# The second block's modulation moved into the first block's attention, and five stores into a mixer

## The chip, the cores and the metric

The kernel runs on one core of a Trainium2 chip. Its time is device microseconds of one execution, from launch to end, as the median of three runs. The profile was taken on a further execution of the same program. TensorE (PE) does the matmuls, VectorE (DVE) and ScalarE (ACT) take the results out of PSUM and do the elementwise work, GpSimd (POOL) helps on data in SBUF, and SyncE (SP) issues the DMA transfers. Each engine works through its own queue in order and waits on semaphores.

## What is computed

Three transformer-like blocks in float32 on 1024 tokens of width 1024. The first block has stick-breaking attention (8 heads of 64) beside a causal pooling, a feed-forward of width 4096 and a per-layer embedding. The second begins with a modulation by a vector c, which is the part that the change moves:

```
# first block
o = stick_breaking_attention(q, k, v)             # sigmoid(z) times a running product of 1 - sigmoid(z)
mixed = concat(rms(o) * g, pooled) @ w_out
x = layer_norm(a * x + mixed)
x = layer_norm(a * x + square(relu(x @ w_up)) @ w_down)
x = layer_norm(a * x + (p @ w_ple) * sigmoid(x @ w_ple_gate))
# second block
mod = silu(c) @ w_ada + b_ada                     # c: 1 x 1024, w_ada: 1024 x 6144
sh_m, sc_m, gt_m, sh_f, sc_f, gt_f = split(mod, 6)
h = rms(x, g_pre_mix) * (1 + sc_m) + sh_m         # first use of mod
...
h = rms(x, g_pre_ffn) * (1 + sc_f) + sh_f
x = x + gt_f * rms(square(relu(h @ w_up)) @ w_down)
```

The third block follows and is not touched.

## The kernel before

The program is a chain of stages, one function each, and all of an engine's instructions stand in the order in which the code writes them; nothing schedules them later. Most matmuls are in three passes on operands split in a high and a low part (lines 130 to 132), with 512 columns moving against 128 x 128 weights.

`embed_attention_1` (from line 3775) does the projections and the attention. The work is cut in 96 parts: a part is 128 queries of one head against up to 512 keys, and parts come in pairs, one for each of two heads. A step of the loop over `i` (a "unit" in the prediction is one part) issues on TensorE, for even `i`, the scores of parts `i` and `i + 1` (line 3961), then the turn, that is the transpose, of part `i - 2` (line 3970), and the values of parts `i - 4` and `i - 3` (line 3981); an odd step has a turn only. Between them, VectorE caps the diagonal block (4201), ScalarE takes two sigmoids (4072, 4073), VectorE scans and multiplies (4210, 4213), and ScalarE copies the turned part out of PSUM (4082). In the first three quarters of the loop, 24 parts each, projections stand between these as well; the last quarter, from part 72, has none. After the loop come two pooled products (3950), the last sums of squares (3990), and the output product in `mix_out_1`.

`feed_forward` (line 529) is the first block's feed-forward in eight parts, each with 8 groups of up and 16 of down. VectorE takes each group out (line 477 for up, 635 for down) and splits operands (119, 124); in the first part it also does the residual of the normalization (253, 254). With `ada` given, GpSimd multiplies w_ada by silu(c) and adds over rows, in 8 column pieces of 768 and two halves each (lines 704 to 716), SyncE loads them (line 557) and stores the eight sums, which still have 128 rows, to HBM.

`per_layer_embedding` (line 1450) loads these sums back and adds their 128 rows on TensorE: 48 matmuls with the ones vector as the single moving column (line 1528), 30 ahead of the first gate product and 18 later; VectorE adds b_ada (1570). VectorE's `take` (1562) multiplies the embedding product (1518) with the gate.

`seven_product_feed_forward` (line 966) does the second block's feed-forward with seven products for eight (Strassen's scheme). Up has 14 pairs of 128 features; the products of a pair are P1, P6, P5, P7, P2, P3, P4, of 12 passes each. VectorE's `w_sums(i)` and `w_low(i)` make the weights of pair `i` (lines 845, 124), `add(i, n)` takes products out and squares them (845, 1196). The first four feature tiles are computed ahead, by `lead_tensor` and `lead_scalar` in the mixer `mix_out_2`. Their blocks and sums are stored to HBM, 14 stores in all (line 988), and `w_sums(1)` waits for all of them, since its scratch lies on two of the blocks. The next chunk of w_up is loaded ahead of these stores (line 995).

Of the kernel before, what the change touches and what calls it, by code (L numbers as in the profile page):

```python
# [5 lines left out]
F32 = mybir.dt.float32  # L6
F32R = mybir.dt.float32r
ALU = mybir.AluOpType
# [3 lines left out]
P = 128  # L12
# [8 lines left out]
ADA = 6 * D // 8  # L21
# [507 lines left out]
def feed_forward(nc, m, F, w_up, w_down, following, tail, x_spill=None, ada=None, split_before=None):  # L529
# [10 lines left out]
    if ada is not None:  # L540
        ada_in, ada_done, ada_out = m.sem("ada_in"), m.sem("ada_done"), m.sem("ada_out")
        ada_step = m.sem("ada_step")
        ada_k = ada.rearrange("(h k p) (j n) -> j h p k n", p=P, h=2, n=ADA)
        ada_w, ada_sum = m.extra[:, 0:4 * ADA].rearrange("p (k n) -> p k n", n=ADA), m.extra[:, 4 * ADA:5 * ADA]
        a_out, m.mod_in = m.mod_spill, m.sem("ple_mod_in")
        m.mod_rows = m.extra[:, 0:5 * ADA].rearrange("p (j n) -> p j n", n=ADA)

    with nc.Block() as block:
        @block.sync
        def _(sp):  # L550
# [4 lines left out]
            def load_ada(j, h):  # L555

                sp.dma_start(ada_w, ada_k[j, h]).then_inc(ada_in, 16)

            def store_ada(j):

                sp.wait_ge(ada_done, 2 * j + 2)
                sp.dma_start(a_out[j], ada_sum).then_inc(ada_out, 16)
            down_dst = F.w_low[1].rearrange("p (k h) n -> p k h n", h=2)
            if ada is not None:
                load_ada(0, 0)
            with sp.Fori(0, parts - 1) as j:
                if ada is not None:
                    sp.wait_ge(ada_done, 2 * j + 1)
                    load_ada(j, 1)
                load(0, base + OUTS * j + UP, F.w_low[0], up_k[:, :, bass.ds(j * COLS + COLS, COLS)])  # L570
                if ada is not None:
                    store_ada(j)
                    load_ada(j + 1, 0)
                load(1, base + OUTS * j + OUTS, down_dst, down_k[j + 1])
            if ada is not None:
                sp.wait_ge(ada_done, 2 * parts - 1)
                load_ada(parts - 1, 1)
                store_ada(parts - 1)
                sp.wait_ge(ada_out, 16 * parts)
                sp.dma_start(m.mod_rows, m.mod_spill[0:5].rearrange("j p n -> p j n")).then_inc(m.mod_in, 16)  # L580
# [115 lines left out]

        if ada is not None:
            @block.gpsimd
            def _(pool):
                def part(j):  # L700
                    for h in range(2):
                        pool.wait_ge(ada_in, 32 * j + 16 * h + 16)
                        c = m.c_act[:, 4 * h:4 * h + 4].unsqueeze(2).broadcast_to([P, 4, ADA])
                        pool.tensor_tensor(ada_w, ada_w, c, ALU.mult).then_inc(ada_step, 1)  # L704
                        pool.wait_ge(ada_step, 5 * j + 2 * h + 1)
                        pool.tensor_tensor(ada_w[:, 0:2], ada_w[:, 0:2], ada_w[:, 2:4], ALU.add).then_inc(ada_step, 1)
                        pool.wait_ge(ada_step, 5 * j + 2 * h + 2)
                        if h == 0:
                            if not (isinstance(j, int) and j == 0):
                                pool.wait_ge(ada_out, 16 * j)  # L710
                            pool.tensor_tensor(ada_sum, ada_w[:, 0], ada_w[:, 1], ALU.add).then_inc(ada_done, 1)
                        else:
                            pool.tensor_tensor(ada_w[:, 0], ada_w[:, 0], ada_w[:, 1], ALU.add).then_inc(ada_step, 1)
                            pool.wait_ge(ada_step, 5 * j + 5)
                            pool.wait_ge(ada_done, 2 * j + 1)
                            pool.tensor_tensor(ada_sum, ada_sum, ada_w[:, 0], ALU.add).then_inc(ada_done, 1)
                part(0)
                with pool.Fori(1, parts) as j:
                    part(j)

class SevenProducts:
# [184 lines left out]

    def lead_vector(self, dve, n):
# [57 lines left out]
def seven_product_feed_forward(nc, m, F, w_up, w_down, following, tail, x_spill):  # L966
# [17 lines left out]
    with nc.Block() as block:  # L984
        @block.sync
        def _(sp):
# [41 lines left out]
            load_chunk(2)  # L1028
            for q in range(2):
                h, pc = F.first_h, F.stage[1]  # L1030
                spill = [F.left_spill[t, q] for t in range(7)]
                sp.wait_ge(F.squared_0, 6 + 2 * q)
                store(F.stored_0, spill[0], h[2 * q][0])
                store(F.stored_0, spill[1], h[2 * q + 1][0])
                store(F.stored_0, spill[2], h[2 * q + 1][1])
# [131 lines left out]
        def _(dve):  # L1167
# [84 lines left out]
            for i in range(F.PAIRS):  # L1252
# [197 lines left out]
def per_layer_embedding(nc, m, a, G, following, V):  # L1450
# [22 lines left out]
    parts_in, mod_done = m.mod_in, m.sem("ple_mod_done")  # L1473
    mod_sets = [(0, 5), (5, 8)]
    mod_rows = m.mod_rows
    n_col = ADA // P
    with nc.Block() as block:
        @block.sync
        def _(sp):
# [5 lines left out]
            sp.wait_ge(mod_done, 1)  # L1485
# [3041 lines left out]
```

## Time and profile before

| | us |
|---|---|
| Median of three runs | 3741.14 |
| Lowest and highest run | 3738.04, 3741.85 |
| Profiled execution | 3736.94 |
| Its span, first to last instruction | 3735.1 |
| TensorE busy in the span | 3520.9 (94%) |
| VectorE busy | 2355.9 (63%) |
| ScalarE busy | 1145.7 (31%) |
| GpSimd busy | 391.6 (10%) |
| Mean granted TensorE clock | 0.972 |

The span is what the profiler saw, the profiled execution's time has the launch and end around it. The granted clock is the share of 2.4 GHz that TensorE got: 1.00 is 2.4 GHz, 0.50 is 1.2 GHz, and a number between is a stretch with both. A matmul's recorded duration is longer than the distance to the next start, because matmuls are pipelined; prices of passes are therefore taken from start to start. "Idle before" in square brackets names what ended an engine's wait.

### The profile page before, as it was taken

To read this page: it belongs to the slowest core of one execution; us is meant where nothing else is said; L and a number is where in the kernel's file an instruction comes from. 1 tells how busy PE (TensorE), PEld (TensorE's weight loads), DVE (VectorE), ACT (ScalarE), POOL (GpSimd) and SP (SyncE) were. 2 spreads that over 40 slices of the span, in tenths; PEclk is the share of its full clock that TensorE was granted. 3 is DMA by queue.
4 is the path that set the end of the run, shared out by engine and by line. 5 is a ranking of instruction groups with operands and counts; after the bars stand their busy time and mean duration, and the time that the engine had idled before them with its cause. 6 is when DMAs were issued, how large, how long until landed. Compare 5 with 4: busy or idle time off the path is not lost. (4 is left out here: it accounts for less than half of the span.)

```text
span 3735.1 us, 42816 instructions
## 1 busy us (share of the span) xinstructions
PE 3520.9 (94%) x16875; PEld 2797.5 (75%) x16875; DVE 2355.9 (63%) x3274; ACT 1145.7 (31%) x2244; POOL 391.6 (10%) x174
## 2 busy tenths in 40 slices
PE   7997898999999989997699999999999999989989
PEld 6664676888888768876677888887777777777687
DVE  7677377555556673999858776768323334446493
ACT  1566230000001352124344224444112223332461
POOL 0113014222331001133100000000000000000000
PEclk9997899999999899999899999999999999999999
DMA  4100212222222121110013436533111221242221
GB/s 168 35 23 23 79 56 84 83 97 109 86 83 99 69 85 54 46 57 23 18 72 125 161 137 216 175 109 145 58 53 60 83 76 59 82 164 97 72 66 76
DMA packets 170935, 323.52 MB, mean 87 GB/s; under 512 B 14992, under 2 KB 45829, under 8 KB 170757
## 3 DMA queue, kind: packets, MB, share of 16 engines
q1 hardware_dynamic: 170756, 321.09, 24.4%
q8 instruction: 119, 1.95, 0.2%
q14 instruction: 60, 0.48, 0.0%
HBM read 248.18 MB, written 72.88 MB: 86 GB/s over the span
## 5 line engine op out<-in xcount | busy, mean ns | idle before, releaser
L130 PE MATMUL banks<-region_parts 128*128 128x512 f32 x2986 | 1195.6, 400 | 40.0 <-DVE region L635 7.5
L132 PE MATMUL banks<-region_parts,weight_chunks_parts 128*128 128x512 f32 x1888 | 739.0, 391 | 0.0
L131 PE MATMUL banks<-region_parts 128*128 128x512 f32 x1802 | 703.8, 391 | 0.0
L130 PEld LDWEIGHTS banks<-region_parts 128*128 128x128 f32 x2986 | 566.8, 190 | 168.3 <-issue 17.9
L132 PE MATMUL banks<-region_parts 128*128 128x512 f32 x1632 | 641.0, 393 | 0.0
L131 PE MATMUL banks<-weight_chunks_parts,region_parts 128*128 128x512 f32 x1536 | 604.7, 394 | 0.0
L132 PEld LDWEIGHTS banks<-region_parts,weight_chunks_parts 128*128 128x128 f32 x1888 | 356.0, 189 | 76.0
L131 PEld LDWEIGHTS banks<-region_parts 128*128 128x128 f32 x1802 | 340.1, 189 | 69.8 <-issue 2.2
L132 PEld LDWEIGHTS banks<-region_parts 128*128 128x128 f32 x1632 | 309.9, 190 | 66.0
L131 PEld LDWEIGHTS banks<-weight_chunks_parts,region_parts 128*128 128x128 f32 x1536 | 293.1, 191 | 63.0 <-issue 4.1
L124 DVE TENSOR_TENSOR region_parts<-region,region_parts 128x512 fp32r<-128x512 f32 (+2 forms) x249 | 266.6, 1072 | 42.1 <-ACT region_parts L848 25.3
L482 ACT ACTIVATE region<-constants 128x512 f32<-128x512 f32 x64 | 40.5, 633 | 618.6 <-DVE constants L477 618.6
L130 PE MATMUL banks<-region_parts,extra_parts 128*128 128x512 f32 x544 | 218.6, 402 | 0.5 <-PEq L984 0.5
L131 PE MATMUL banks<-region_parts,extra_parts 128*128 128x512 f32 x544 | 212.5, 391 | 0.0
L124 DVE TENSOR_TENSOR weight_chunks_parts<-weight_chunks,region_parts 128x1024 fp32r<-128x1024 f32 (+5 forms) x88 | 197.0, 2238 | 2.3
L3220 POOL TENSOR_TENSOR constants<-mask,blocks 128x128 f32<-128x128 f32 x24 | 11.0, 484 | 1672.0 <-DMA b_gate<-in_b_gate 1575.1
L635 DVE TENSOR_TENSOR region<-region,banks 128x512 f32<-128x512 f32 x128 | 85.5, 684 | 148.9 <-PE banks L132 148.6
L2708 DVE CUSTOM_DVE_ANT_0 region<-banks,region 128x128 f32<-128x128 f32 (+7 forms) x64 | 48.5, 758 | 189.9 <-PE banks L2623 135.7
L848 ACT ACTIVATE region_parts<-region 128x512 fp32r<-128x512 f32 (+2 forms) x190 | 118.6, 660 | 145.3 <-DMA region<-left_spill 96.7
L4210 DVE TENSOR_TENSOR_SCAN region<-region,small_numbers 128x512 f32<-128x512 f32 (+3 forms) x96 | 111.6, 1162 | 61.9 <-ACTq L4075 61.9
L1962 DVE SCALAR_TENSOR_TENSOR region<-region,columns 128x1023 f32<-128x1023 f32 (+29 forms) x120 | 149.2, 1330 | 0.0
L704 POOL TENSOR_TENSOR extra<-extra,silu_c 128x3072 f32<-128x3072 f32 x16 | 86.8, 5424 | 570.2 <-DMA extra<-in_w_ada 570.2
(432 smaller groups left out, 5205.3 us busy)
## 6 DMA issues: line engine op xcount, KB each, us to landing
weight_chunks<-in_w_in SPq DMA_DIRECT2D x19, 2048.0 KB, 8.4
weight_chunks<-in_w_up SPq DMA_DIRECT2D x16, 2048.0 KB, 9.3
region<-left_spill SPq DMA_DIRECT2D x98, 256.0 KB, 2.6
extra<-in_w_ada SPq DMA_DIRECT2D x16, 1536.0 KB, 10.8
weight_chunks<-in_w_down SPq DMA_DIRECT2D x9, 2048.0 KB, 7.7
x_spill<-region SPq DMA_DIRECT2D x32, 512.0 KB, 2.6
weight_chunks<-in_w_out SPq DMA_DIRECT2D x8, 2048.0 KB, 8.0
region<-x_spill SPq DMA_DIRECT2D x32, 512.0 KB, 6.2
```

The lines of the kernel that those rows point to most:

```text
L124: return dve.tensor_tensor(m.parts(x), x, m.parts(hi).bitcast(F32), ALU.subtract)
L130: pe.matmul(out, m.parts(lhs[0]), m.parts(rhs[0]), start=first, stop=False, skip_group_check=shared)
L131: pe.matmul(out, m.parts(lhs[0]), m.parts(rhs[1]), start=False, stop=False, skip_group_check=shared)
L132: return pe.matmul(out, m.parts(lhs[1]), m.parts(rhs[0]), start=False, stop=last, skip_group_check=shared)
L482: act.activation(self.h_place(self.h_low, g), self.relu_of, ACT.Square).then_inc(self.squared, 1)
L635: dve.tensor_tensor(x, x, m.bank[:, g % NBANK, :], ALU.add).then_inc(wt.bank_free, 1)
L704: pool.tensor_tensor(ada_w, ada_w, c, ALU.mult).then_inc(ada_step, 1)
L848: act.activation(self.m.parts(hi), x, ACT.Copy).then_inc(sem, 1)
L1962: dve.scalar_tensor_tensor(y, val[:, k, 0:S - lag], m.c("w_dw", (CONV_W - 1 - lag) * 4 + k), y, op0=ALU.mult, op1=ALU.add).then_inc(tap, 1)
L2708: m.dve_link(dve, dve.tensor_tensor_reduce(SB[n % 2][:, 0:w], src, logc[:, (7 - t) * P:(7 - t) * P + w], 1.0, -3e38, ALU.add, ALU.max, x[: ...
L3220: ins = pool.tensor_tensor(bd[t].rearrange("p (b d) -> p b d", d=4), m.mask4.unsqueeze(2).broadcast_to([P, 32, 4]), m.blk[:, t, k:k + 1, : ...
L4210: dve.tensor_tensor_scan(x, x, zeros.broadcast_to([P, w]), kb[:, at + w:at + w + 1], ALU.mult, ALU.add).then_inc(s.scanned, 1)
```

## The change

The modulation leaves the feed-forward and the per-layer embedding. In the attention, w_ada is loaded in 24 pieces of 1024 x 256 into three buffers, one in `extra` and two in the half of the weight buffer that is free by then. A piece is 16 matmuls of 128 x 128 weights with silu(c), 128 x 1, as the moving column, two accumulations of 8. Two pieces stand behind the scores of every even step from part 78 on, four in the last step. VectorE adds b_ada and the gains in one go at the end of the loop, and the last pooled product waits for that, since it uses the same bank. In the second block's feed-forward five of the 14 stores are issued at the end of the mixer, the load of the next chunk of w_up comes behind the other nine, and `w_sums(1)` stands behind `add(0, 2)` instead of ahead of it.

```diff
 def feed_forward(...):          # and all of ada's loads, stores and the block below
-        if ada is not None:
-            @block.gpsimd
-            def _(pool):
-                def part(j):
-                    for h in range(2):
-                        pool.wait_ge(ada_in, 32 * j + 16 * h + 16)
-                        c = m.c_act[:, 4 * h:4 * h + 4].unsqueeze(2).broadcast_to([P, 4, ADA])
-                        pool.tensor_tensor(ada_w, ada_w, c, ALU.mult).then_inc(ada_step, 1)
...
 def per_layer_embedding(...):   # TensorE; DVE's modulation(0), modulation(1) go as well
-            modulation(0)
             for q in range(G.LEAD, 16):
...
-                if q == 5:
-                    modulation(1)
 class SevenProducts:
+    def lead_sync(self, sp):
+        for squares, tile, half in ((1, 0, 0), (2, 1, 0), (3, 2, 0), (4, 3, 0), (6, 1, 1)):
+            sp.wait_ge(self.squared_0, squares)
+            sp.dma_start(self.left_spill[2 if half else tile % 2, tile // 2], self.first_h[tile][half]).then_inc(self.stored_0, 16)
 def mix_out_2(...):             # SyncE
             wt.load(sp, m.wbuf, following[1])
+            F.lead_sync(sp)
 def seven_product_feed_forward(...):
-            load_chunk(2)
             for q in range(2):
...
+            load_chunk(2)
...
                 if i == 0:
                     F.t_low_part(dve, 1, 0, 4)
-                    F.w_sums(dve, 1)
                 add(i, 2)
                 if i == 0:
+                    F.w_sums(dve, 1)
                     F.w_low(dve, 1, range(4))
 def embed_attention_1(...):
+    ADA_BUFS, ADA_PIECES, ADA_FROM = 3, 24, 78
...
+    for n in range(ADA_PIECES):
+        at = ADA_FROM + n // 2 * 2 if n < 22 else NP + 4 - 2
+        ada_at.setdefault((at, 0), []).append(n)
...                              # SyncE, after piece 0 and, once the projections are done, 1 and 2
+            for n in range(ADA_BUFS, ADA_PIECES):
+                sp.wait_ge(s.ada_done, n - ADA_BUFS + 1)
+                load_ada(n)
+            sp.wait_ge(s.ada_done, ADA_PIECES)
             wt.load(sp, m.wbuf, following[1])
...                              # TensorE
+            def modulation(n):
+                if n == 0:
+                    pe.wait_ge(s.c_ready, 1)
+                    pe.wait_ge(wt.bank_free, NBANK + 38)
+                pe.wait_ge(s.ada_in[n % ADA_BUFS], 16 * (n // ADA_BUFS + 1))
+                for t in range(2):
+                    for k in range(NK):
+                        mm = pe.matmul(m.bank[:, 3, 2 * n + t:2 * n + t + 1], ada_w[n % ADA_BUFS][:, k, t * P:(t + 1) * P],
+                                       m.c_act[:, k:k + 1], start=(k == 0), stop=(k == NK - 1), skip_group_check=True)
+                mm.then_inc(s.ada_done, 1)
...
                 if i < NP and i % 2 == 0:
                     scores(i)
                     scores(i + 1)
+                for n in ada_at.get((i, 0), []):
+                    modulation(n)
                 if 2 <= i < NP + 2:
                     turn(i - 2)
...
-            for half in range(2):
-                pooled(3, half, 38 + half)
+            pooled(3, 0, 38)
+            pe.wait_ge(s.mod_read, 1)
+            pooled(3, 1, 39)
...                              # VectorE, after the loop
+            dve.wait_ge(s.ada_done, ADA_PIECES)
+            dve.tensor_tensor(m.mod, m.bank[:, 3, 0:48], m.cols("b_ada", 0, 48), ALU.add).then_inc(s.mod_read, 1)
```

On TensorE, two steps of the attention's last quarter, parts 90 to 93, stood so before (L3961 are scores, L3970 turns, L3981 values; x8 are eight matmuls in a row):

```order
L3961 MATMUL banks<-region 128x512 x2
L3970 MATMUL banks<-constants,region 128x128 x3
L3981 MATMUL banks<-region 64x128 x8
L3970 MATMUL banks<-constants,region 128x128 x3
L3961 MATMUL banks<-region 128x512 x2
L3970 MATMUL banks<-constants,region 128x128 x4
L3981 MATMUL banks<-region 64x128 x6
L3970 MATMUL banks<-constants,region 128x128 x4
```

Now, in the same two steps (the lines have moved up: L3904 scores, L3913 turns, L3924 values, L3937 the modulation):

```order
L3904 MATMUL banks<-region 128x512 x2
L3937 MATMUL banks<-silu_c,extra 128x1 x16
L3937 MATMUL banks<-silu_c,weight_chunks 128x1 x16
L3913 MATMUL banks<-constants,region 128x128 x3
L3924 MATMUL banks<-region 64x128 x8
L3913 MATMUL banks<-constants,region 128x128 x3
L3904 MATMUL banks<-region 128x512 x2
L3937 MATMUL banks<-silu_c,weight_chunks 128x1 x16
L3937 MATMUL banks<-silu_c,extra 128x1 x16
L3913 MATMUL banks<-constants,region 128x128 x4
L3924 MATMUL banks<-region 64x128 x6
L3913 MATMUL banks<-constants,region 128x128 x4
```

32 matmuls of one column stand between the scores and the turn in each step, and the rest is as it was.

On VectorE, at the start of the second block's feed-forward, the low part of the fourth sum was followed by `w_sums(1)` (four L845 on weight_chunks), then by `add(0, 2)` with its square (L845, L1196):

```order
L124 TENSOR_TENSOR region_parts<-region,region_parts 128x4x512
L845 TENSOR_TENSOR extra<-weight_chunks 128x512
L845 TENSOR_TENSOR weight_chunks<-weight_chunks 128x4x128
L845 TENSOR_TENSOR region<-weight_chunks 128x512
L845 TENSOR_TENSOR extra<-weight_chunks,region 128x512
L845 TENSOR_TENSOR region<-region,banks 128x512
L1196 SCALAR_TENSOR_TENSOR region<-region 128x512
L124 TENSOR_TENSOR weight_chunks_parts<-weight_chunks,region_parts 128x8x256
```

Now the same operations stand so (L123, L790 and L1145 are these lines):

```order
L123 TENSOR_TENSOR region_parts<-region,region_parts 128x4x512
L790 TENSOR_TENSOR region<-region,banks 128x512
L1145 SCALAR_TENSOR_TENSOR region<-region 128x512
L790 TENSOR_TENSOR extra<-weight_chunks 128x512
L790 TENSOR_TENSOR weight_chunks<-weight_chunks 128x4x128
L790 TENSOR_TENSOR region<-weight_chunks 128x512
L790 TENSOR_TENSOR extra<-weight_chunks,region 128x512
L123 TENSOR_TENSOR weight_chunks_parts<-weight_chunks,region_parts 128x8x256
```

The add and its square went ahead of the four sums, and the sums now stand next to the low part that uses them.

## Rows read from the trace of the kernel before

**Rows 1.** Windows: stretch, its length, busy time (pieces) of PE, PEld, DVE, ACT, POOL, PEclk.
```profile
331.10:396.30 65.20, 40.52 (x246) 22.39 (x245) 45.66 (x50) 42.53 (x74) 23.07 (x9) 0.73 0.00 1
700.00:800.00 100.00, 100.00 (x443) 82.81 (x442) 52.18 (x47) 5.70 (x9) 25.62 (x7) 1.00 0.28 105
```
**Rows 2.** Waits of PE, 331 to 396.3: total us, times, longest.
```profile
PE banks L3970 <- DVE region L4213: 7.3, 7, 2.5
```
**Rows 3.** Timeline, PE and DVE around L1528: start, us, engine, line, [idle before].
```profile
1262.26 0.77 PE L130 MATMUL banks<-region_parts 128*128 128x512 f32 x1
...
1266.67 0.49 PE L131 MATMUL banks<-weight_chunks_parts,region_parts 128*128 128x512 f32 x1
...
1275.19 0.69 DVE L1562 TENSOR_TENSOR region<-region,banks 128x512 f32<-128x512 f32 x1 [4.44 <-PE banks L1518]
...
1287.24 4.46 PE L1528 MATMUL banks<-constants,extra 128*128 128x1 f32 x36
1291.56 3.76 PE L1518 MATMUL banks<-region 128*128 128x512 f32 x4
```
**Rows 4.** Line L1528, weight loads: ns min/median/max, first and last start.
```profile
L1528 PEld LDWEIGHTS banks<-constants,extra x96: 186/192/338, 1251.2 to 1291.3; 128*128 128x128 f32 x96
```
**Rows 5.** Timeline, PEld: weight loads of L1528 in three stretches.
```profile
1251.23 1.86 PEld L1528 LDWEIGHTS banks<-constants,extra 128*128 128x128 f32 x16 [1.58 <-issue]
...
1253.87 8.44 PEld L1528 LDWEIGHTS banks<-constants,extra 128*128 128x128 f32 x39
...
1287.02 3.77 PEld L1528 LDWEIGHTS banks<-constants,extra 128*128 128x128 f32 x32
```
**Rows 6.** Windows, PEld on L1528 alone: busy (pieces), PEclk, DMA share, GB/s.
```profile
1251.20:1253.10 1.90, 1.87 (x17) 1.00 0.29 87
1253.35:1262.20 8.85, 8.85 (x43) 0.50 0.58 215
```
**Rows 7.** Timeline, PE, one step of part 90, and the last values.
```profile
371.68 2.08 PE L3961 MATMUL banks<-region 64*128 64x512 f32 x4 [2.95 <-ACT region L4073]
373.69 0.90 PE L3970 MATMUL banks<-constants,region 128*128 128x128 f32 x3
374.52 1.79 PE L3981 MATMUL banks<-region 128*64 128x128 f32 x16
...
395.22 1.10 PE L3981 MATMUL banks<-region 128*64 128x128 f32 x16 [0.69 <-ACT region L4082]
```
**Rows 8.** DMA issues, 500 to 1200: count, KB each, us to landing.
```profile
extra<-in_w_ada SPq DMA_DIRECT2D x16, 1536.0 KB, 10.8
```
**Rows 9.** Timeline, POOL and DVE at the first feed-forward's start.
```profile
540.66 6.57 POOL L704 TENSOR_TENSOR extra<-extra,silu_c 128x3072 f32<-128x3072 f32 x1 [158.52 <-DMA extra<-in_w_ada]
...
542.58 5.73 DVE L253 SCALAR_TENSOR_TENSOR region<-region,gain_offset 128x1024 f32<-128x1024 f32 x1
...
555.99 1.22 DVE L253 SCALAR_TENSOR_TENSOR region<-region,gain_offset 128x1024 f32<-128x1024 f32 x1
...
558.96 0.69 DVE L124 TENSOR_TENSOR region_parts<-region,region_parts 128x512 fp32r<-128x512 f32 x1
...
563.14 5.71 DVE L124 TENSOR_TENSOR region_parts<-region,region_parts 128x512 fp32r<-128x512 f32 x1
```
**Rows 10.** Waits of PE, 533 to 640: total us, times, longest.
```profile
PE banks L130 <- DVE region L635: 7.5, 2, 5.8
PE banks L130 <- DVE constants L477: 5.5, 1, 5.5
```
**Rows 11.** Windows, after the first stop (columns as in rows 1).
```profile
569.40:574.50 5.10, 4.99 (x12) 3.72 (x12) 5.07 (x3) 0.63 (x1) 5.02 (x2) 0.55 0.00 0
```
**Rows 12.** Timeline, DVE and PE at the second block's feed-forward's start.
```profile
2014.84 0.69 DVE L845 TENSOR_TENSOR extra<-weight_chunks 128x512 f32<-128x512 f32 x1 [7.44 <-DMA left_spill<-extra]
...
2018.45 0.76 PE L130 MATMUL banks<-region_parts 128*128 128x512 f32 x1 [5.83 <-DVE region L845]
...
2021.75 1.29 DVE L124 TENSOR_TENSOR extra_parts<-extra,region_parts 128x512 fp32r<-128x512 f32 x2
```

More of the change, by code:

```diff
@@ L20 @@
 D_FF = 4096
-ADA = 6 * D // 8
 ALPHA = float(2.0 ** 0.25)
@@ L695, in _ @@
             tail.scalar(act)
-        if ada is not None:
-            @block.gpsimd
-            def _(pool):
-                def part(j):
-                    for h in range(2):
-                        pool.wait_ge(ada_in, 32 * j + 16 * h + 16)
-                        c = m.c_act[:, 4 * h:4 * h + 4].unsqueeze(2).broadcast_to([P, 4, ADA])
-                        pool.tensor_tensor(ada_w, ada_w, c, ALU.mult).then_inc(ada_step, 1)
[L705 to L719, printed above, removed]
 class SevenProducts:
@@ L1520, in ple @@
                 mm.then_inc(ple_done, 1)
-            def modulation(n):
-                j0, j1 = mod_sets[n]
-                pe.wait_ge(parts_in, 16 * n + 16)
-                for j in range(j0, j1):
-                    for i in range(n_col):
-                        mm = pe.matmul(m.bank[:, 7, n_col * j + i:n_col * j + i + 1], mod_rows[:, j - j0, i * P:(i + 1) * P],
-                                       m.ones[:, 0:1], start=True, stop=True, skip_group_check=True)
-                mm.then_inc(mod_done, 1)
             TURN_BEFORE = {8: 0, 10: 1, 12: 2, 14: 3}
             pe.wait_ge(G.early.x_low, NT)
-            modulation(0)
             for q in range(G.LEAD, 16):
@@ L1565, in take @@
                 dve.sem_inc(gated, 1)
-            def modulation(n):
-                c0, c1 = n_col * mod_sets[n][0], n_col * mod_sets[n][1]
-                dve.wait_ge(mod_done, n + 1)
-                m.dve_link(dve, dve.tensor_tensor(m.mod[:, c0:c1], m.bank[:, 7, c0:c1], m.cols("b_ada", c0, c1 - c0), ALU.add))
-                at, g = ((8, "g_pre_mix"), (32, "g_pre_ffn"))[n]
-                part = m.mod[:, at:at + 8]
-                m.dve_link(dve, dve.scalar_tensor_tensor(part, part, 1.0, m.cols(g, 0, 8), op0=ALU.add, op1=ALU.mult))
             residual = m.norm_2.residual
@@ L1579, in _ @@
                 residual(dve, i)
-            modulation(0)
             for q in range(4):
@@ L1588, in _ @@
                 take(q)
-                if q == 4:
-                    modulation(1)
                 if c == 1:
@@ L3867, in embed_attention_1 @@
     w_pair = a.w_in.rearrange("(k p) (s j n) -> s j p k n", p=P, s=4, n=P)
+    ADA_BUFS, ADA_PIECES, ADA_FROM = 3, 24, 78
+    w_ada = a.w_ada_2.rearrange("(k p) (c n) -> c p k n", p=P, n=2 * P)
+    slot_0 = m.wbuf[:, 0].rearrange("p k n -> p (k n)")
+    ada_w = [t[:, b * 2 * S:(b + 1) * 2 * S].rearrange("p (k n) -> p k n", n=2 * P) for t, b in ((ex, 0), (slot_0, 0), (slot_0, 1))]
+    s.c_ready, s.ada_done, s.mod_read = m.sem("a1_c_ready"), m.sem("a1_modulation_done"), m.sem("a1_modulation_read")
+    s.ada_in = [m.sem(f"a1_w_modulation_in_{b}") for b in range(ADA_BUFS)]
+    ada_at = {}
+    for n in range(ADA_PIECES):
+        at = ADA_FROM + n // 2 * 2 if n < 22 else NP + 4 - 2
+        ada_at.setdefault((at, 0), []).append(n)
     with nc.Block() as block:
@@ L3899, in _, with load_ada @@
             wt.load(sp, m.wbuf, following[0])
+            def load_ada(n):
+                sp.dma_start(ada_w[n % ADA_BUFS], w_ada[n]).then_inc(s.ada_in[n % ADA_BUFS], 16)
+            sp.wait_ge(wt.mm_done, number[2, 5] + 1)
+            load_ada(0)
             sp.wait_ge(wt.mm_done, 36)
+            for n in range(1, ADA_BUFS):
+                load_ada(n)
             for i in range(4):
                 sp.dma_start(hi[:, 4 + i, :], a.x0_spill[i]).then_inc(m.x_again, 16)
+            for n in range(ADA_BUFS, ADA_PIECES):
+                sp.wait_ge(s.ada_done, n - ADA_BUFS + 1)
+                load_ada(n)
+            sp.wait_ge(s.ada_done, ADA_PIECES)
             wt.load(sp, m.wbuf, following[1])
@@ L4009, in _ @@
                     scores(i + 1)
+                for n in ada_at.get((i, 0), []):
+                    modulation(n)
                 if 2 <= i < NP + 2:
                     turn(i - 2)
+                for n in ada_at.get((i, 1), []):
+                    modulation(n)
                 if i < NP:
@@ L4269, in _ @@
                     mixes += 1
+            dve.wait_ge(s.ada_done, ADA_PIECES)
+            dve.tensor_tensor(m.mod, m.bank[:, 3, 0:48], m.cols("b_ada", 0, 48), ALU.add).then_inc(s.mod_read, 1)
+            dve.wait_ge(s.mod_read, 1)
+            for at, g in ((8, "g_pre_mix"), (32, "g_pre_ffn")):
+                part = m.mod[:, at:at + 8]
+                dve.scalar_tensor_tensor(part, part, 1.0, m.cols(g, 0, 8), op0=ALU.add, op1=ALU.mult)
             while mixes < len(groups):
```

46 lines of the change are left out of this document (6 added, 40 removed).

## The prediction

> **What bounds the kernel now.** I read the page's lines of busy time and its 40 slices first, then the windows of the four places that the diff touches, and for each of them the waits and the timeline. In a dense stretch TensorE is busy throughout and starts a 512-column pass every 0.226 us (443 in 100 us) [rows 1]; there the time is TensorE's, and a faster helper is worth nothing unless TensorE was waiting for it. Where the modulation is to go, the last quarter of the first block's attention, it is different: of 65.2 us TensorE is busy for 40.5, at a mean granted clock of 0.73 [rows 1]. Its waits there, of which the largest stands in [rows 2], are for VectorE's products and for ScalarE: a pair of units goes through scores, cap, sigmoids, scan, product, turn, copy and values, and each engine waits for the one before. That idle time is where the added work would hide.
>
> **The passes that are added.** w_ada has 8 x 48 blocks of 128 x 128, and each becomes the stationary operand of a matmul with one moving column: 384 matmuls, 24 pieces of 16. In the kernel before, 18 such matmuls of L1528 are recorded as 36 passes [rows 3], each with a weight load; so 768 passes are added. One load lasts 0.19 us in the median and up to 0.34 [rows 4]. The price is from start to start [rows 5]: the first 16 take (1.86 - 0.19) / 15 = 0.111 us, and 39 later ones (8.44 - 0.33) / 38 = 0.213 us. The granted clock was 1.00 in the one stretch and 0.50 in the other [rows 6]. They run without a gap, so the clock level alone doubles the price: 768 passes are 85 us at 2.4 GHz and 164 us at 1.2 GHz. And they let the clock fall: before it fell, TensorE had left its dense 512-column passes and issued one-column passes only; it rose again when dense work had run from 1262.3 to 1266.7 us, where the length of a pass drops [rows 3].
>
 The rows agree at the upper level and not at the lower, so the measurement decides. By the page's figure the passes would be an estimated 82 us and the total an estimated 3,759 us.
>
> **What of it hides.** On TensorE the order per even step becomes scores, two pieces, turn, values, turn. TensorE is one queue, so all that stands behind the pieces waits for them, and ScalarE and VectorE for that. The 18 units from the 78th on took 65.2 us in nine steps, 7 us each; two pieces alone are 64 passes, 7.1 us at the upper level and 13.7 at the lower. So the waits of this stretch vanish under the pieces, and it becomes TensorE's own work plus the passes. The own work is the 40.5 us: in one step at the lower level 2.0 us of scores, 0.8 of turns before the values and 1.7 of values [rows 7]. The last four pieces stand behind the last scores, where nothing covers them.
>
> For the clock I count steps. In the second group of L1528 32 passes ran at the upper price before it rose [rows 5], in the first 17. A step's own matmuls last 4 to 5 us at the lower level, about what brought the clock back after 1262.3; so I let it recover in six or seven of eleven steps, with some 25 passes each at the upper level: 170 of 768. That is 170 x 0.111 + 598 x 0.213 = 146.3 us. The stretch becomes 146.3 + 40.5 = 186.8 us instead of 65.2: **+121.6 us**. Bounds: all passes at the lower level and the own work slowed to about 46 us, 164 + 46 - 65.2 = +145; all at the upper, own work 40.5 x 0.73 = 29.6, 85 + 29.6 - 65.2 = +49.
>
> The pieces' loads cost nothing beside that: a load of 1,536 KB took 10.8 us in the median [rows 8], a piece is 1,024 KB, and three buffers give it two pieces and a step's own work, over 13 us at the lower level. If that cover were gone, each piece would add the few us that remain. The second load of output weights waits for the last piece and, as before, for the last pooled product, so it isn't later against the end of the stage. VectorE's three small operations on the modulation stand ahead of its last mix and are over before the last values end.
>
> **What is removed in the first feed-forward.** GpSimd's products over w_ada go. They slowed VectorE: L253 took 1.22 us beside an idle GpSimd and 5.73 when it began 1.9 us into GpSimd's product of 6.57 us, ending about 1 us after it; an L124 of 0.69 us took 5.71 later [rows 9]. In its first 45 us here VectorE falls some 20 us behind by such operations (seven of them, two shown), TensorE finds no free bank and stands still for 5.5 and 5.8 us [rows 10]. After each stop the clock is low: twelve passes fill the 5.1 us of [rows 11], 4.9 us instead of 12 x 0.226 = 2.7, and about as much after the second stop, another 2.2 + 1.9. Without GpSimd VectorE needs 4.3 us per group of outputs (two residual operations of 1.22, and three of 0.4 to 0.7) against TensorE's 24 x 0.226 = 5.4, so nothing takes the place of these stops. A third stop, the 1.7 us that remain of the 7.5 in [rows 10], comes after a slowed L124 as well. Sum 11.3 + 4.1 + 1.7: **-17 us**; bounds 0, if VectorE stays late for another reason, and -20, all of its delay.
>
> **In the per-layer embedding** the one-column matmuls leave TensorE. The 11 us of the first group are not all won: VectorE works on residuals and weights that don't change until 4.4 us before 1275.2, and the first take, which then waits for TensorE [rows 3], needs those residuals. After the change it can start 4.8 us earlier, the 0.4 us of modulation before the wait included; TensorE will have stood idle by then, so some of its next passes will be at the lower level: I take -3. The second group is on TensorE's own line: 36 passes, 4.3 us up to the next start, and behind it four passes of L1518 at the lower level, 2.8 us up to the next line instead of 1.7, and some 1.5 us more in the product after them [rows 3]. Together **-10 us**, bounds -6 and -13.
>
> **In the second block's feed-forward** the first pair's weight sums wait for 14 stores that queue behind a load of 2 MB: VectorE stood 7.4 us before L845 at 2014.8, and TensorE 5.8 us for the add that stands behind the sums [rows 12]. Now five stores go ahead in the mixer, the load comes after the others, and the add stands ahead of the sums. TensorE had come to 2012.6 without a stop, so its fourth product ends two products of 12 passes earlier, at 2007.1; VectorE, free from 2007.4, has the add and its square done at 2008.8. The nine stores should be down by then. The weights are ready 2023.0 - 2014.8 = 8.2 us after the sums begin, less part of the 1.4 us of add and square that lay between, say 7.6: 2016.4. Before, the next pair began behind twelve passes at the lower level from 2018.45, at 2023.6, and was slow for another 0.4 us. **-7.6 us**; bounds 0, if the stores land late, and -8.6. The load that now goes last is needed a pair later.
>
> **Sum.** The profiled execution took 3736.9 us (span 3735.1), 4.2 under the median of the three runs and 1.1 under the lowest. 3736.9 + 121.6 - 17 - 10 - 7.6 = 3823.9, about **3824 us**.
>
> **Rivals.** *The clock stays up.* If the other matmuls between the pieces keep it at 2.4 GHz, the stretch grows by 49 us and the total is 3736.9 + 49 - 34.6 = 3751. If only the passes kept the upper price, with the own work as it is, it would be 85 + 40.5 - 65.2 = 60 and 3763. For it: half of the stretch before was at the upper level. Against it: 64 one-column passes in a row are more than the 17 or 32 that the clock bore. (The page's rule cited above would put the time in this case.) *The clock stays down:* +145, total 3847. For it: the stretch had only 0.73 with no one-column pass in it. *The passes hide* (the other side): with the clock up, own work leaves 65.2 - 29.6 = 35.6 us of room, and 34.6 are won elsewhere, so a gain needs 70.2 / 768 = 0.091 us per pass or less. A shorter pass stands here only for 64-column weights: 16 passes of the values in 1.10 us [rows 7], about 0.055 start to start. At that price the stretch grows by 42 + 29.6 - 65.2 = 7 and the total is 3709. Against it: L1528 was never under 0.111. *The gains don't come:* if VectorE in the feed-forward and the stores stay late, the total is up to 24.6 us higher, 3848.
>
> **Chances.** Forecast, 3805 to 3838: 0.62. Clock down or gains missing, to 3855: 0.17. The clock more often up, 3765 to 3805: 0.10. Clock up, 3751 to 3763: 0.06. Hidden, 3709: 0.05. The range 3785 to 3851 holds the first, most of the second and half of the third. A measurement of this kernel tells 0.2% (7.5 us) from no change; faster by more has 0.05, within it 0.03 (the low edge of the clock-up case), slower 0.92.
>
> **What would show it.** Right: from the 78th unit to the last values some 187 us, one-column passes back to back at two prices, TensorE's waits near nothing, granted clock near 0.6; in the feed-forward no GpSimd work and no stop of TensorE near its start; one gap fewer in the embedding and in the second block's feed-forward. Wrong: one-column passes under 0.1 us, a granted clock near 1 through the pieces, waits for the pieces' loads, or 5 us operations of VectorE still in the feed-forward.

## The result, and the profile after

The kernel after takes **3846.6 us** (median of four runs, 3844.5 to 3850.9), 1.0283 times the kernel before (95% interval 1.0265 to 1.0301): slower by 2.8%. The forecast was 3824 with a range of 3785 to 3851, so the sign and the range held and the point was 22.6 us low. The profiled execution has a span of 3843.4 us, 108.3 more than before.

To see where the time went I matched the dense 512-column matmuls of both traces in their order, which is the same, and read how much later each starts. The lag is constant over long stretches; the table has the value of each (the time in the trace of before in brackets, all figures rounded by themselves):

| up to | lag of after, us | change, us | forecast, us |
|---|---|---|---|
| end of the first block's attention (400) | 138.2 | +138.2 | +121.6 |
| start of the first feed-forward (512 to 564) | 135.9 | -2.3 | 0 |
| its first group of outputs over (from 606) | 118.1 | -17.8 | -17 |
| the embedding's one-column passes over (from 1298) | 105.3 | -12.8 | -10 |
| start of the second block's feed-forward (to 2012) | 107.7 | +2.4 | 0 |
| its second pair running (from 2025) | 99.9 | -7.8 | -7.6 |
| end | 108.2 | +8.4 | 0 |

The quarter of the attention, as a window (columns as in [rows 1], then DMA share and GB/s); before, it took 65.2 us with 40.52 busy:

```profile
331.00:535.00 204.00, 202.10 (x1015) 181.23 (x1015) 40.27 (x53) 42.96 (x74) 21.01 (x9) 0.54 0.34 109
```

TensorE no longer waits: 1.9 us in 204. VectorE and ScalarE do the work of before in three times the time. The clock fell from a mean of 0.73 to 0.54. TensorE's timeline of two steps (start, us, engine, line, operation, count):

```profile
366.32 1.12 PE L3913 MATMUL banks<-constants,region 128*128 128x128 f32 x4
367.37 1.51 PE L3904 MATMUL banks<-region 64*128 64x512 f32 x4
368.81 11.31 PE L3937 MATMUL banks<-silu_c,weight_chunks 128*128 128x1 f32 x64
379.98 0.45 PE L3913 MATMUL banks<-constants,region 128*128 128x128 f32 x1
380.36 1.98 PE L3924 MATMUL banks<-region 128*64 128x128 f32 x16
```

Sixteen values passes take 1.98 us here, 1.79 at 374.52 before and 1.10 where the clock was up [rows 7]: the attention's own matmuls became slower too. The 64 passes of L3937 in between run at both prices, as that line alone shows in two windows (length, busy time and pieces of PE, the same of PEld, granted clock, DMA share, GB/s), the answer to [rows 6]:

```profile
368.80:371.50 2.70, 2.69 (x24) 2.69 (x25) 1.00 0.00 0
371.70:379.90 8.20, 8.20 (x40) 8.20 (x40) 0.50 0.40 128
```

Over all 768, start to start: 135 at 0.112 us and 621 at 0.213, the rest across the ends of steps. All 768 together are some 150 us. In these two windows the DMA share differs as well as the clock, 0.00 and 0.40; that the loads aren't what doubles the price is seen below, where passes keep 0.112 us at a share of 0.57.

In the first feed-forward the stretch of [rows 10] now lies from 669 to 758 us. TensorE's only wait in it is this one; the 7.5 and 5.5 us are gone:

```profile
PE banks L129 <- PEq L367: 0.5, 1, 0.5
```

VectorE's operation of [rows 9] that took 5.73 us is never over its own time there (L252 now: busy us, mean ns):

```profile
L252 DVE SCALAR_TENSOR_TENSOR region<-region,gain_offset 128x1024 f32<-128x1024 f32 x8 | 9.7, 1217 | 0.0
```

In the embedding, VectorE's first take (L1492) starts without a wait, behind its residuals, 4.9 us earlier than the lag of 118.0 would put it, as the forecast had it (4.8); the 4.44 us of [rows 3] are gone. TensorE now waits for the loads of w_ple and for that take:

```profile
1387.11 1.23 DVE L253 SCALAR_TENSOR_TENSOR region<-gain_offset,region 128x1024 f32<-128x1024 f32 x1
1388.37 0.69 DVE L1492 TENSOR_TENSOR region<-region,banks 128x512 f32<-128x512 f32 x1
```

```profile
PE banks L1451 <- DMA region<-in_w_ple: 2.4, 1, 2.4
PE banks L1461 <- DVE region L1492: 2.1, 1, 2.1
```

In the second block's feed-forward the sums begin at 2116.33 with no wait, where [rows 12] had 7.44, and the last low parts are ready at 2123.8, 7.5 us after the sums begin (the forecast had 7.6):

```profile
2115.72 0.69 DVE L1145 SCALAR_TENSOR_TENSOR region<-region 128x512 f32<-128x512 f32 x1
2116.33 0.69 DVE L790 TENSOR_TENSOR extra<-weight_chunks 128x512 f32<-128x512 f32 x1
...
2119.73 2.29 DVE L123 TENSOR_TENSOR weight_chunks_parts<-weight_chunks,region_parts 128x2048 fp32r<-128x2048 f32 x1 [0.53 <-ACT region_parts L793]
...
2122.54 1.28 DVE L123 TENSOR_TENSOR extra_parts<-extra,region_parts 128x512 fp32r<-128x512 f32 x2
```

### The profile page after: what moved, and what is told of

Its sections match the earlier page's. It is cut to its first block and busy times, and to the rows that moved or that the text cites. A ratio compares the mean times of both kernels' runs of the same rounds, so it can differ in the third digit from the quotient of the medians.

```text
span 3843.4 us, 43964 instructions
## 1 busy us (share of the span) xinstructions
PE 3656.6 (95%) x17547; PEld 2934.3 (76%) x17547; DVE 2240.6 (58%) x3273; ACT 1146.0 (30%) x2244; POOL 182.7 (5%) x118
## 5 line engine op out<-in xcount | busy, mean ns | idle before, releaser
L123 DVE TENSOR_TENSOR region_parts<-region,region_parts 128x512 fp32r<-128x512 f32 (+2 forms) x249 | 215.4, 866 | 45.7 <-ACT region_parts L793 28.9
L123 DVE TENSOR_TENSOR weight_chunks_parts<-weight_chunks,region_parts 128x1024 fp32r<-128x1024 f32 (+5 forms) x88 | 186.2, 2116 | 2.8 <-ACT region_parts L793 0.5
L4169 DVE TENSOR_TENSOR_SCAN region<-region,small_numbers 128x512 f32<-128x512 f32 (+3 forms) x96 | 110.8, 1154 | 121.6 <-ACTq L4034 121.6
L476 DVE TENSOR_SCALAR constants<-banks 128x512 f32<-128x512 f32 x64 | 44.2, 690 | 189.9 <-PE banks L131 178.1
L129 PE MATMUL banks<-extra_parts,region_parts 128*128 128x512 f32 x320 | 128.3, 401 | 10.1 <-DVE region_parts L123 10.1
```

Of the source, the lines that this page charges most:

```text
L123: return dve.tensor_tensor(m.parts(x), x, m.parts(hi).bitcast(F32), ALU.subtract)
L129: pe.matmul(out, m.parts(lhs[0]), m.parts(rhs[0]), start=first, stop=False, skip_group_check=shared)
L476: dve.tensor_scalar(self.relu_of, m.bank[:, g % NBANK, :], 0.0, None, ALU.max).then_inc(m.wt.bank_free, 1)
L4169: dve.tensor_tensor_scan(x, x, zeros.broadcast_to([P, w]), kb[:, at + w:at + w + 1], ALU.mult, ALU.add).then_inc(s.scanned, 1)
```

## Experiments

Theory: the loss is the added passes alone, their price is set by the clock level, and their single columns let the clock fall; the gains elsewhere are those of VectorE no longer held up by GpSimd, of the passes taken out of the embedding, and of the stores. Rivals: the price doesn't hang on the clock; the place in the step or the loads cost; the gains are given back.

**Without the pieces.**

```diff
-                for n in ada_at.get((i, 0), []):
-                    modulation(n)
...
-            dve.tensor_tensor(m.mod, m.bank[:, 3, 0:48], m.cols("b_ada", 0, 48), ALU.add)...
+            dve.tensor_copy(m.mod, m.cols("b_ada", 0, 48))...
```

(and no load of w_ada)

> The kernel after without the 24 loads and the 384 one-column matmuls: c @ w_ada is left out, the modulation is b_ada and the gains only. The feed-forward and store edits stay. Theory (the whole loss is the added passes in the attention's last quarter, which grew by 138 us in the trace): the last quarter is back at some 65 us, TensorE's waits for VectorE and ScalarE with it, and the total is 3846.6 - 138 = 3708, give or take 6. Rival (part of the gain in the feed-forward and the embedding, 38 us in the trace, was only waiting that the later attention made up, or moving the loads and the buffers costs by itself): 3715 to 3740. The 8 us that the untouched late stages lost in the trace of after: if they come from the removed edits' new phase of the clock, they are here too; if from the passes, they go and the total is nearer 3700.

Measured: 3704.9 us, 0.9913 of before (0.9898 to 0.9928). From 1.0283 that is 3.70% of 3739, 138 us, as much as the attention grew; by the two intervals it is known to some 9 us. The quarter's window is that of [rows 1] again:

```profile
331.00:396.00 65.00, 41.33 (x237) 22.79 (x238) 45.74 (x53) 42.70 (x74) 23.04 (x9) 0.71 0.00 1
```

The late stages still lose 4.6 us against before in its trace, so not all of the 8.4 come with the passes.

**64 and 128 moving columns in place of one.**

```diff
-   m.bank[:, 3, 2 * n + t:2 * n + t + 1] ... m.c_act[:, k:k + 1]
+   m.bank[:, 3, 2 * n + t:2 * n + t + 64] ... m.cols("c", k, 64)
```

(silu of c stands in the place of c among the columns; 128 likewise)

> The kernel after with 64 moving columns in place of one in each of the 384 matmuls (the other 63 results are overwritten by later columns or never read); the same weights are loaded, so TensorE is given strictly more to do. Theory (the price of a pass is set by the clock level, and one-column passes let the clock fall): the clock stays up for most of the quarter, a pass costs some 0.11 us, the own work shrinks to 30 to 40 us, the quarter takes 115 to 135 us instead of 203 and the total is 3846.6 - 80 = about 3765. Rival 1 (a pass behind a weight load costs 0.21 us whatever the clock, and the low clock is a sign, not a cause): granted clock up, but the total within 10 us of 3847. Rival 2 (64 columns add their own time): the total above 3847, by up to 768 x 0.03 = 23 us.

> The kernel with 64 moving columns once more, for a second trace. Theory: where the total is near 3787, some stretch of the pieces ran at the lower level, at 0.213 us a pass; 27 us more are some 260 passes. Rival: the pieces are as in the first trace and the time is lost elsewhere.

> The kernel after with 128 moving columns in place of one. With 64 the pieces took 0.112 us a pass in the profiled run, but the timed runs stood 25 to 38 us above it, and at a lower mean clock. Theory (the clock alone sets the price, and with 64 columns it fell in some runs): with 128 it stays up in each, the timed runs agree with the profiled one, 3752 to 3765. Rival 1 (columns cost time of their own now: 128 columns need more than the weight load beside them): over 3765 in every run with the clock up. Rival 2 (what made the timed runs longer is not the pieces' clock): the spread stays.

The traces with 64 columns have spans of 3757.8 and 3758.7 us, 85 less than after, though TensorE is given 64 times the columns in the pieces. Of the 768 passes 748 start within 0.15 us of the one before, 0.1115 us in the mean, and the attention grows by 55 us in place of 138. The window of the first trace:

```profile
331.00:451.00 120.00, 117.22 (x1006) 103.20 (x1006) 42.40 (x54) 42.52 (x74) 22.10 (x10) 0.98 0.57 185
```

The weight load is the same instruction on the same data in both kernels; its median is 0.333 us with one column and 0.192 with 64, here on the line L3937 (ns min/median/max), of after and then of 64 columns:

```profile
L3937 PEld LDWEIGHTS banks<-silu_c,weight_chunks x512: 186/333/338, 339.8 to 531.3; 128*128 128x128 f32 x171
```

```profile
L3937 PEld LDWEIGHTS banks<-columns,weight_chunks x512: 186/192/192, 337.3 to 450.3; 128*128 128x128 f32 x171
```

So the clock is cause, not sign, and up to 128 columns beside a weight load cost nothing here (0.112 us a pass with 1, 64 and 128 at the upper level). The Trainium skill, "TensorE: Matmul & The Clock Gate", section "LDWEIGHTS (loading the stationary operand)", gives a load as its columns over 1.2 GHz, an estimated 107 ns for 128 columns, and names no clock level with it. By these runs that is near the price at 2.4 GHz, 0.112 us from start to start, and half of that at 1.2 GHz, 0.213.

Measured with 64 columns: 3786.6 us, 1.014 (1.0125 to 1.0156), above the 3765 that I expected. The timed runs were less even than the traces: 3760 and then 3784 to 3798, at mean clocks of 0.981 and 0.970 to 0.972. With 128 columns: 3761.6, 1.0066 (1.0051 to 1.0082); all four lie between 3760.3 and 3763.2, at 0.979 to 0.981, and in the trace 730 passes start at 0.112 us and 24 at 0.213. That fits a clock that fell in some runs with 64, but no trace caught one of these: the second trace was a run of 3760.5 like the first. What made the longer runs stays open.

**The pieces behind the turn.**

```diff
-        ada_at.setdefault((at, 0), []).append(n)
+        ada_at.setdefault((at, 1), []).append(n)
```

> The kernel after with the two pieces of a step put behind the turn and not ahead of it. Theory (the stretch is TensorE's own line, passes plus own work, with hardly a wait): the place in the step doesn't matter, 3847 give or take 6. Rival (the pieces ahead of the turn delay the chain through ScalarE and VectorE, whose waits of TensorE for a turn's operands then cost): faster by 10 us or more, with TensorE's waits for VectorE's products gone.

> The kernel after, unchanged, beside the others. It tells apart two readings of the 11.6 us by which the kernel with the pieces behind the turn was under it, and of the 8.4 us that its late stages lost in the first trace. Theory (both are the clock's low stretches that fall differently from run to run, not the place of the pieces): 3835 to 3850, with some runs near 3835, and late stages in the second trace that differ from the first by several us. Rival (the place of the pieces is worth 11 us): 3844 to 3850 in every run.

Measured: 3835.1 us, 1.0256 (1.024 to 1.0271); the kernel after again, 3844.5 (3836.1 to 3850.6), 1.0281 (1.0265 to 1.0296). My 3847 give or take 6 was missed, but the intervals overlap, and after itself ran once in 3836. The attention grew by 136.5 us with the pieces behind the turn, by 138.2 and 143.1 in the two traces of after, in the order in which the clock gave passes at the upper price: 149, 135 and 112. TensorE's waits for VectorE, which the rival wanted gone, did not go. Of TensorE from 300 to 560 us, after and then behind the turn:

```profile
PE banks L3944 <- ACT region L4049: 7.2, 3, 3.4
PE banks L3913 <- DVE region L4172: 3.3, 3, 1.6
```

```profile
PE banks L3944 <- ACT region L4049: 6.1, 3, 2.5
PE banks L3913 <- DVE region L4172: 3.5, 4, 1.6
```

So the waits are not what the place changes. The medians are some 9 us apart, the clock's passes at the upper price account for 2 to 7 of it in the traces, and whether the place decides how many of these there are is not settled. The late stages of the second trace lost 7.6 us, the first's 8.4: that half of my expectation, that they would differ by several us, was missed.

**One matmul of eight, all loads.**

```diff
-                    for k in range(NK):
+                    for k in range(1):
```

> The kernel after with one of each eight matmuls of the pieces: all 24 loads, waits and positions stay, 48 matmuls or 96 passes in place of 768; seven eighths of the sum over c @ w_ada are left out. Theory (only the passes cost, the loads and waits nothing): 96 passes of 0.11 to 0.21 us are 10 to 20 us, part of them in TensorE's waits of the quarter; 3705 + 0 to 20, about 3712. Rival (the 25 MB of loads, or the chain of piece, load and next piece, hold the stretch by themselves): the quarter stays over 100 us, with waits of TensorE for the pieces' loads, and the total is above 3740.

Measured: 3718.0 us, 0.9949 (0.9932 to 0.9966), 13 us over the kernel without pieces, as expected; but the reason isn't the passes alone. In its quarter the DMA engines are busy for 0.84 of the time, and TensorE waits for the loads:

```profile
331.00:413.00 82.00, 65.51 (x343) 44.44 (x342) 44.97 (x54) 42.59 (x74) 24.07 (x10) 0.62 0.84 269
```

```profile
402.74 0.60 PE L3937 MATMUL banks<-silu_c,extra 128*128 128x1 f32 x4 [0.81 <-DMA extra<-in_w_ada]
406.84 1.01 PE L3937 MATMUL banks<-silu_c,weight_chunks 128*128 128x1 f32 x4 [3.49 <-DMA weight_chunks<-in_w_ada]
409.61 1.01 PE L3937 MATMUL banks<-silu_c,weight_chunks 128*128 128x1 f32 x4 [1.76 <-DMA weight_chunks<-in_w_ada]
```

The attention grew by 17.5 us. With one pass in eight the loads are the next bound: 0.84 of 82 us is 69 us of loading, more than the 65.2 of the quarter, so no shorter pass could have hidden the modulation wholly where its loads are placed now.

**The stores alone, on the kernel before.**

```diff
+            F.lead_sync(sp)          # in the mixer: five stores
-            load_chunk(2)            # ahead of the other stores
+            load_chunk(2)            # behind them
```

(with the add ahead of the sums)

> The kernel before with one part of the change alone: the five stores moved into the mixer, the weight load put behind the others, and the add put ahead of the second pair's weight sums. Theory: the gain of the second block's feed-forward stands alone, -7.4 us as in the trace, 3734. Rival (the gain is given back in the later stages, which lost 8.4 us in the trace of after, because the clock's low stretches shift with the new phase): 3738 to 3743, no difference.

Measured: 3731.7 us, 0.9982 (0.9973 to 0.9991), 7.0 us less than before's 3738.7: the term of the forecast, by itself.

**Later products of GpSimd, on the kernel before.**

```diff
+                pool.wait_ge(wt.mm_done, base + UP + 6)
                 part(0)
```

(and the load of w_up ahead of SP's wait for GpSimd)

> The kernel before, with GpSimd's products over w_ada begun later: GpSimd waits until 6 products of the first feed-forward's first output group are done, and the queue of loads issues the next weights ahead of its wait for GpSimd. Nothing else is changed; the modulation is still computed there. Theory (TensorE's stops at the start of the feed-forward came from VectorE's operations slowed beside GpSimd while VectorE had no room; the products themselves cost nothing later): the 17 us of the forecast, 18 in the trace of after, come without moving any work to TensorE, 3738.7 - 17 = 3722. Rival (the stops only move to where GpSimd begins now): 3736 to 3742, with waits of TensorE for a bank some 30 us later.

Measured: 3733.2 us, 0.9986 (0.9977 to 0.9995), only 4.6 us, between the expectation and its rival. In the trace the 14 to 16 us are won by 585 us, and 9 of them are lost again by 620. VectorE's residual operations, which had been short, met the second product of GpSimd:

```profile
591.61 5.31 POOL L704 TENSOR_TENSOR extra<-extra,silu_c 128x3072 f32<-128x3072 f32 x1 [6.84 <-DMA extra<-in_w_ada]
```

```profile
590.22 1.22 DVE L254 SCALAR_TENSOR_TENSOR region<-gain_offset,region 128x1024 f32<-128x1024 f32 x1
591.48 1.28 DVE L635 TENSOR_TENSOR region<-region,banks 128x512 f32<-128x512 f32 x2
592.68 5.32 DVE L253 SCALAR_TENSOR_TENSOR region<-region,gain_offset 128x1024 f32<-128x1024 f32 x1
```

L253 was issued at 592.68 and ended at 598.00: 1.1 us after the product ended at 596.92, about its own time of 1.22. TensorE's waits for VectorE's outputs, from 533 to 640 us, are these:

```profile
PE banks L130 <- DVE region L635: 6.7, 2, 3.9
```

**64 columns in the embedding, on the kernel before.**

```diff
-   m.bank[:, 7, x:x + 1] ... m.ones[:, 0:1]
+   m.bank[:, 7, x:x + 64] ... m.ones[:, 0:64]
```

(x stands for `n_col * j + i`)

> The kernel before, with 64 moving columns in place of one in the 48 matmuls of the modulation in the per-layer embedding. Theory (the clock falls with one-column passes and sets their price): they keep 2.4 GHz, 96 passes at 0.111 us take 10.7 us and the dense passes around them are not slowed; the first group gains little, since VectorE is not ready before 1271, the second some 4 us: 3738.7 - 5, between -3 and -9. Rival (what the change won in the embedding was the passes themselves and not the clock): no change, 3736 to 3742.

Measured: 3735.3 us, 0.9992 (0.9983 to 1.0001), 2.5 us: too small to tell from nothing in the timed runs. In its trace the embedding gives back 4.9 us (a lag of 1.2 becomes -3.7).

**The three together**, and the same with GpSimd only behind the third product of the second group of outputs:

```diff
-                pool.wait_ge(wt.mm_done, base + UP + 6)
+                pool.wait_ge(wt.mm_done, base + OUTS + 3)
```

> The kernel before with the three: stores in the mixer and the add ahead of the weight sums, GpSimd's products begun later, and 64 moving columns in the embedding's modulation. The whole computation is done, and no pass is added to TensorE. Theory (the gains of the change need none of its added passes, and add up): -7 -17 -5, 3738.7 - 29 = 3710, within 10 us of the kernel after without its pieces (3705). Rival (the gains overlap or are given back by the clock): 3718 to 3730.

> As the kernel with the three edits (stores in the mixer, later products of GpSimd, 64 columns in the embedding), but GpSimd begins only behind the third product of the second group of outputs, when VectorE has done its last residual operation, and the next loads of weights go ahead of the wait for GpSimd there. Nothing is left out. Theory (in the trace of the first try the feed-forward had won 13.7 us at 580 us and gave 8 back from 592 us on, when GpSimd met VectorE's last residual operations: 5.32 us in place of 1.22): those 8 us stay won, and the total is 3720 - 8 = 3712. Rival (GpSimd beside VectorE costs them wherever it begins, here in the second group's splitting of the weights and outputs): 3716 to 3722, with waits of TensorE for a bank near 640 us.

Measured: 3720.0 us, 0.9953 (0.9939 to 0.9967), and 3716.7, 0.9944 (0.993 to 0.9957). Both are below both kernels, by 0.5% to 0.6% of before; between the two the intervals overlap. The three gains come to less than the 29 us that I expected, because those of GpSimd and of the embedding were smaller: 7.0, 4.6 and 2.5 us by themselves, 14.1, and 17.7 together. The later start moved the collision again, so the rival's range was right and its place, near 640 us, was not. Its trace had won 17.4 us at 660 and 7.9 at 700, after these (GpSimd first, then VectorE, then TensorE's waits from 600 to 720):

```profile
673.57 6.59 POOL L714 TENSOR_TENSOR extra<-extra,silu_c 128x3072 f32<-128x3072 f32 x1 [6.88 <-DMA extra<-in_w_ada]
680.23 7.56 POOL L716 TENSOR_TENSOR extra<-extra 128x1536 f32<-128x1536 f32 x1
```

```profile
675.02 9.41 DVE L124 TENSOR_TENSOR weight_chunks_parts<-weight_chunks,region_parts 128x4096 fp32r<-128x4096 f32 x1
684.36 2.47 DVE L645 TENSOR_TENSOR region<-region,banks 128x512 f32<-128x512 f32 x4
```

```profile
PE banks L130 <- DVE region_parts L124: 4.5, 1, 4.5
PE banks L130 <- DVE region L645: 2.1, 1, 2.1
```

L124 alone takes 4.42 us. Issued 1.45 us into GpSimd's product, it ended at 684.43, 4.3 us after the product ended at 680.16; and the sum behind it on GpSimd, 3.5 us elsewhere, ended 3.4 us after L124. By these times each stood still until the other was done. The Trainium skill, "SBUF — State Buffer", section "SBUF: two separate sides", says so of a VectorE operation with two inputs in SBUF beside one of GpSimd: the pair of ports that they share is an exclusive lock for a whole instruction, and whoever comes second blocks fully. These rows agree.

## Why the prediction was right in sign, and 22.6 us low

*TensorE's own line: right.* The stretch became passes plus own work, 202.1 busy of 204 us, and taking the passes away gives 138 us back.

*The price of the passes: right.* 0.112 and 0.213 us against 0.111 and 0.213. (Where the forecast says that 32 passes of L1528 ran at the upper price "before it rose", the rows show the clock falling there.) *The share at the upper level: a little high.* I let the clock recover in six or seven steps of eleven, with 25 passes each, 170 in all; it rose five times, for 22 to 30 passes each, 135 in all. Passes: 150 us, not 146.3.

*The own work: mis-sized, the term that failed.* "Own work 40.5" was TensorE's busy time at a mean clock of 0.73 [rows 1], and I kept it while forecasting a lower clock. What remains of the stretch is 65.2 + 138.2 - 150 = 53 us. Counted in the trace, TensorE's other instructions fill 52.4 us of it (54.7 in the second trace of after). Scaled by the clock, 40.5 x 0.73 / 0.54 = 54.8, the term would have been right within 3 us. With 64 columns the same scaling gives 40.5 x 0.73 / 0.98 = 30, and the trace 65.2 + 55 - 85.6 = 35, of which some 2 are idle (32.8 counted). The forecast's bound of "about 46" at the lower level was too low for the same reason: 40.5 x 0.73 / 0.50 is 59. This term and the passes are 16.6 of the 22.6 us; the late stages, below, are most of the rest.

*The loads: right here, for a reason that the forecast gave and a price it left vague.* They cost nothing beside passes at the lower level; beside few passes they hold the stretch.

*The first feed-forward: right*, -17.8 for -17, and so was its cause: the stops went with GpSimd's products. These are harmless where VectorE has room: from 606 to 1250 us the lag stays at 118, though only the kernel before has GpSimd at work there. By the two later starts they cost some 9 us where they meet a long operation of VectorE or come when it has no room.

*The embedding: about right*, -12.8 and -11.1 in the two traces of after, for -10. The first group keeps 5.4 and 3.7 us of its 11, not 3. *The second block's feed-forward: right*, -7.8 for -7.6.

*What the forecast did not have:* the stages behind it, which nobody edited, lost 8.4 us in one trace of after and 7.6 in the other. In the others of the change's kernels they lost 4.6 to 5.7, but 1.2 with one matmul of eight; in those of the kernel before's 1.2 to 3.0. TensorE has the same 6852 matmuls there; in the first trace of after 4.7 of the 8.4 us are busy time and the rest longer waits, mostly for the same things, and the granted clock was low for 65 us in place of 54. Whether any edit does it, or the traces merely differ, is not settled.

*The rivals.* That the clock stays down had 3847, closest to the time; its condition was nearly met (81% of the passes at the lower level), but its +145 was not reached, and the late stages made up the rest. That it stays up gave 3751, and the kernel in which it does, with 128 columns, 3761.6: the mechanism was right and its condition was not met. That the passes hide fell twice, by the price and by the loads.

## What to carry to other kernels

When an edit lowers the clock, scale all of TensorE's work in the stretch by the clock's ratio, not only the added work. A stream of one-column matmuls can be bought at twice its price: here 128 columns on the same weights cost no more at the upper level, held the clock there for nearly all passes of the trace and gave even times in all four runs, where 64 did so in the traced runs only. Before work goes to the engine that bounds the kernel, ask whether it can stay where it was at another time, and look there for the other engine's longest operation.

## What I had not expected of the hardware

Sixty-four times the columns made the kernel 85 us shorter in the traces (60 in the medians): most passes of 1 column took 0.213 us and nearly all of 64 or 128 columns 0.112, since the clock stood at 1.2 GHz for the one and at 2.4 for the others. And VectorE and GpSimd block each other in both directions: a product of GpSimd held a VectorE operation of 4.42 us for 9.41, and that held GpSimd's next sum of 3.5 us for 7.56.
